# A fixed group of four dense fp32 matmuls at the start of each RWKV scan of a hybrid FNet / RWKV-7 step

## The chip, the cores and the metric

The kernel runs on one core of one Trainium2 chip. The metric is the device time of one execution in microseconds (us). Three runs of the kernel before gave 3294.38, 3295.61 and 3301.01 us; the median is 3295.61 us.

## The reference, cut to what matters

One layer is computed for two streams, 1024 latent tokens and 128 prompt tokens, with a model width of 1024: norm, SwiGLU FFN, norm, mixer, norm, FFN, final norm. The mixer has a Fourier half and an RWKV-7 half of 8 heads with 64 features each. The RWKV half is a recurrence over the tokens, forward and backward:

```python
def step(state, inp):
    r_t, w_t, k_t, v_t, kk_t, a_t = inp
    sa = jnp.einsum('bhvk,bhk->bhv', state, -kk_t)
    state = (state * w_t[:, :, None, :]
             + sa[..., None] * (kk_t * a_t)[:, :, None, :]
             + v_t[..., None] * k_t[:, :, None, :])
    return state, jnp.einsum('bhvk,bhk->bhv', state, r_t)
```

The kernel returns both streams' outputs and the final prompt states of both directions.

## The kernel before, in words

The program is a row of stages with a barrier between them: load, modulation, FFN 0, mixer projection, Fourier, RWKV, mixer output, FFN 1, output. RWKV (`rwkv`, L1838) takes the 8 heads in four pairs. For each pair `rw_chunks` (L1461) turns the recurrence into 18 chunks of 64 tokens, `rw_scan` (L1712) runs through the chunks one after the other, and `rw_turn` (L1329) normalises and gates the result and makes the operands of the next pair. The first three pairs are the body of a hardware loop with `more=True`; the fourth stands behind it with `more=False`.

In `rw_scan` both directions d = 0, 1 go through chunks i = 0 to 17 together. TensorE's program per chunk is: `s_part(i, 0)` and `s_part(i, 1)` (L1740: two 64x64 matmuls each, the heads' states times a chunk factor), then `rest(i, 0)` and `rest(i, 1)` (L1749, L1754, L1758: two matmuls each for the new state and four for the output). Every fp32 matmul call stands as two MATMUL instructions in the trace. `s_part` waits for the states of the chunk before (VectorE, L1791) and for ScalarE to have copied the outputs of the chunk before out of PSUM (L1813). `rest` waits for VectorE's sum (L1784). GpSimd multiplies the old state by the decay (L1804) for VectorE's L1791. At i = 0 `s_part` waits for the memset of the states, L1779.

With `more`, class `Prep` prepares the next pair inside the scan: after the chunk's `rest(i, 1)` TensorE runs item i - 1 of a list. The first item, `ss`, is `head_sums` (L1137): nine calls with 128x128 weights and two moving columns. It waits for ScalarE's `sq` (L1230), which follows `kraw` (L1228), which waits for a load and for `ka1` on VectorE (L1255). On VectorE `prep.dve` comes after the chunk's L1791, and on ScalarE `prep.act` comes after the chunk's L1813. The further items are matmuls with 384 moving columns (L1216) and 128x128 ones (L1145). PSUM banks 6 and 7 belong to these items in the scan; the matmuls of the scan itself write banks 0 to 5. Nothing reads bank 7 before the item that writes it.

Of the kernel before, what the change touches and what calls it, by code (L numbers as in the profile page):

```python
# [14 lines left out]
P = 128  # L15
# [31 lines left out]
C_ID, C_MASK, C_ONE, C_BLK, C_CLS = 0, 128, 384, 512, 640  # L47
# [25 lines left out]
def fresh(name, count=count()):  # L73

    return f"{name}{next(count)}"
# [48 lines left out]
def mm3(pe, out, w_hi, w_lo, x_hi, x_lo, start, stop):  # L124

    pe.matmul(out, w_lo, x_hi, start=start, stop=False)  # L126
    pe.matmul(out, w_hi, x_lo, start=False, stop=False)  # L127
    return pe.matmul(out, w_hi, x_hi, start=False, stop=stop)  # L128


def parts(c):
# [1580 lines left out]
def rw_scan(nc, io, sb, rw, zd, p, more):  # L1712
# [6 lines left out]
    with Stage(nc) as st, nc.psum_tensor(fresh("c_ps"), [P, 8, 512], F32) as ps:  # L1719
        pe_t = Steps(st.sem("pe_s"), [x for i in range(NCH) for x in (f"S{i}_0", f"S{i}_1", f"M{i}_0", f"Y{i}_0", f"M{i}_1", f"Y{i}_1")] +  # L1720
                     ["st0", "st1"])
        dve_t = Steps(st.sem("dve_s"), ["zero"] + [x for i in range(NCH) for x in
                                                   [f"S{i}_0", f"S{i}_1"] + [f"M{i}_0", f"M{i}_1"]])
        act_t = Steps(st.sem("act_s"), [f"Y{i}_{d}" for i, d in SD] + ["st0", "st1"])
        pool_t = Steps(st.sem("pool_s"), [f"mp{i}_{d}" for i, d in SD])
        out_s = st.sem("out_s")
        prep = Prep(st, io, sb, rw, zd, p + 1, ps[:, 6:8, :]) if more else None
        old = lambda i, d: rw.m0[:, d, :] if i == NPC else rw.m[:, i % 2, d, :]
        with st.block() as block:
            @block.tensor  # L1730
            def _(pe):

                def s_part(i, d):
                    c = order[d][i]
                    dve_t.wait(pe, f"M{i - 1}_{d}" if i else "zero")
                    if i:
                        act_t.wait(pe, f"Y{i - 1}_{d}")
                    for h in range(2):
                        rows = slice(HS * h, HS * h + HS)
                        last = pe.matmul(ps[0:HS, 2 * d + h, 0:HS], rw.ar[rows, d, 0, c * HS:(c + 1) * HS],  # L1740
                                         old(i, d)[rows], start=True, stop=True)
                    pe_t.did(f"S{i}_{d}", last)

                def rest(i, d):
                    c = order[d][i]
                    dve_t.wait(pe, f"S{i}_{d}")
                    for h in range(2):
                        rows = slice(HS * h, HS * h + HS)
                        last = pe.matmul(ps[rows, 4 + d, 0:HS], rw.bt[:, d, c, HS * h:HS * h + HS],  # L1749
                                         rw.sv[:, d, h, c, :], start=True, stop=True)  # L1750
                    pe_t.did(f"M{i}_{d}", last)
                    for h in range(2):
                        rows = slice(HS * h, HS * h + HS)
                        pe.matmul(ps[rows, 2 * d + h, HS:2 * HS], rw.sv[:, d, h, c, :], rw.gr[:, d, h, c, HS:2 * HS],  # L1754
                                  start=True, stop=False)
                    for h in range(2):
                        rows = slice(HS * h, HS * h + HS)
                        last = pe.matmul(ps[rows, 2 * d + h, HS:2 * HS], old(i, d)[rows],  # L1758
                                         rw.ar[rows, d, 1, c * HS:(c + 1) * HS], start=False, stop=True)
                    pe_t.did(f"Y{i}_{d}", last)  # L1760
                for i, d in SD:
                    s_part(i, d)
                    if d:
                        rest(i, 0)
                        rest(i, 1)
                        if more:
                            prep.pe(pe, i)
                for d in range(2):

                    act_t.wait(pe, f"Y{NCH - 1}_{d}")  # L1770
                    for h in range(2):
                        rows = slice(HS * h, HS * h + HS)
                        last = pe.matmul(ps[rows, 2 * d + h, HS:2 * HS], rw.st[rows, d, :],
                                         sb["cst"][rows, C_ID + HS * h:C_ID + HS * h + HS], start=True, stop=True)
                    pe_t.did(f"st{d}", last)

            @block.vector
            def _(dve):
                dve_t.did("zero", dve.memset(rw.m[:, 0, :, :], 0.0))  # L1779
                for i in range(NCH):  # L1780
                    for d in range(2):
                        c = order[d][i]
                        pe_t.wait(dve, f"S{i}_{d}")
                        dve_t.did(f"S{i}_{d}", dve.tensor_tensor(rw.sv[0:HS, d, :, c, :], ps[0:HS, 2 * d:2 * d + 2, 0:HS],  # L1784
                                                                 rw.gr[0:HS, d, :, c, 0:HS], ALU.add))
                    for d in range(2):
                        c = order[d][i]
                        new = rw.st[:, d, :] if i == NPC - 1 else rw.m[:, (i + 1) % 2, d, :]
                        pe_t.wait(dve, f"M{i}_{d}")
                        pool_t.wait(dve, f"mp{i}_{d}")  # L1790
                        dve_t.did(f"M{i}_{d}", dve.scalar_tensor_tensor(new, ps[:, 4 + d, 0:HS], rw.pc[:, d, c:c + 1],  # L1791
                                                                       rw.mp[:, d, :], ALU.mult, ALU.add))
                    if more:
                        prep.dve(dve, i)

            @block.gpsimd
            def _(pool):
                for i, d in SD:
                    c = order[d][i]
                    if i:  # L1800
                        dve_t.wait(pool, f"M{i - 1}_{d}")
                    else:
                        dve_t.wait(pool, "zero")
                    pool_t.did(f"mp{i}_{d}", pool.tensor_scalar(rw.mp[:, d, :], old(i, d), rw.pc[:, d, c:c + 1], None, ALU.mult))  # L1804

            @block.scalar
            def _(act):
                for i, d in SD:
                    c = order[d][i]
                    pe_t.wait(act, f"Y{i}_{d}")  # L1810
                    for h in range(2):
                        rows = slice(HS * h, HS * h + HS)
                        last = act.activation(y[d][rows, c * HS:(c + 1) * HS], ps[rows, 2 * d + h, HS:2 * HS], ACT.Copy)  # L1813
                    act_t.did(f"Y{i}_{d}", last)
                    if more and d:
                        prep.act(act, i)
                for d in range(2):
                    pe_t.wait(act, f"st{d}")
                    dve_t.wait(act, f"M{NCH - 1}_{d}")
                    for h in range(2):  # L1820
                        rows = slice(HS * h, HS * h + HS)
                        last = act.activation(rw.mp[rows, d, :], ps[rows, 2 * d + h, HS:2 * HS], ACT.Copy)
                    act_t.did(f"st{d}", last)

            @block.sync
            def _(sp):
                if more:
                    prep.sync(sp)
                    for sem in prep.z_in + prep.w_in:
                        sp.wait_ge(sem, 16)  # L1830
                for d, name in enumerate(("state_f", "state_b")):
                    act_t.wait(sp, f"st{d}")
                    sp.dma_start(io[name][0, 0, bass.ds(p * 2, 2), :, :].rearrange("h v k -> (h v) k"), rw.mp[:, d, :])\
                      .then_inc(out_s, 16)
                sp.wait_ge(out_s, 32)
# [129 lines left out]
```

## Time and profile before

| | |
|---|---|
| median of the three runs | 3295.61 us |
| the runs | 3294.38 to 3301.01 us |
| span of the profiled execution, first to last instruction | 3298.7 us |
| TensorE matmul busy (PE) | 2845.0 us, 86% |
| VectorE busy (DVE) | 1469.7 us, 45% |
| ScalarE busy (ACT) | 782.5 us, 24% |
| mean granted clock of TensorE | 0.850 of full |

No separate time is given for the profiled execution. Its span, 3298.7 us, lies 3.1 us above the median and inside the runs' own spread, so what lies around the span is not told apart here, and sums are made as differences. In the profile PE is TensorE's matmuls, PEld its weight loads, PEclk the granted clock as a share of full speed (1.0 is 2.4 GHz, 0.5 is 1.2 GHz). Matmuls are pipelined: the duration of one has a tail that the next one overlaps, so the pace is read from the starts.

### The profile page before, as it was taken

How to read it: one execution, taken by the hardware profiler on the slowest of the kernel's cores; microseconds unless marked ns; L12 is line 12 of the kernel's file. 1: busy time of each engine (PE TensorE's matmuls, PEld its weight loads, DVE VectorE, ACT ScalarE, POOL GpSimd, SP SyncE). 2: the span in 40 equal slices, each digit the busy share in tenths (PEclk: the TensorE clock that was granted, in tenths of full speed). 3: DMA queues.
4: the chain of work that ended last, by engine and by line, in shares of the span. 5: the costliest groups of instructions: out<-in, count | busy, mean ns of one | idle time of the engine just before them, and what ended most of it. 6: DMA issues, size and time to landing. Idle time of an engine off the chain costs nothing. (4 is left out here: it accounts for less than half of the span.)

```text
span 3298.7 us, 47247 instructions
## 1 busy us (share of the span) xinstructions
PE 2845.0 (86%) x18910; PEld 2646.2 (80%) x18910; DVE 1469.7 (45%) x2799; ACT 782.5 (24%) x1527; POOL 105.5 (3%) x165
## 2 busy tenths in 40 slices
PE   4589999999995999578679678686879999999995
PEld 2289999999995998266476565665879999999995
DVE  1453333333437661372563745723364433333335
ACT  1231111112104111333233433322141111111112
POOL 0000000000000000001102001010000000000000
PEclk8799999999997999665665755757989999999997
DMA  8511111111101223110010110104111111111101
GB/s 342 211 52 39 38 38 49 40 45 45 45 0 40 95 82 112 68 28 26 18 23 24 25 39 3 30 9 161 33 51 45 42 40 38 38 38 51 38 19 58
DMA packets 190797, 182.67 MB, mean 55 GB/s; under 512 B 43955, under 2 KB 163550, under 8 KB 190686
## 3 DMA queue, kind: packets, MB, share of 16 engines
q1 hardware_dynamic: 190416, 180.97, 17.0%
q8 instruction: 86, 1.41, 0.2%
q14 instruction: 25, 0.20, 0.0%
q10 hardware_dynamic: 270, 0.09, 0.0%
HBM read 153.05 MB, written 27.98 MB: 55 GB/s over the span
## 5 line engine op out<-in xcount | busy, mean ns | idle before, releaser
L126 PE MATMUL ff_ps<-h_hi,ff_wlo 128*128 128x384 f32 x2112 | 710.7, 336 | 12.2 <-ACT ff_s L591 7.7
L127 PE MATMUL ff_ps<-h_lo,ff_whi 128*128 128x384 f32 x2112 | 709.4, 336 | 0.0
L128 PE MATMUL ff_ps<-h_hi,ff_whi 128*128 128x384 f32 x2112 | 709.1, 336 | 0.0
L126 PEld LDWEIGHTS ff_ps<-h_hi,ff_wlo 128*128 128x128 f32 x2112 | 399.9, 189 | 13.4 <-issue 8.2
L639 DVE TENSOR_TENSOR ff_s<-ff_ps,ff_s 128x384 f32<-128x384 f32 x132 | 73.6, 557 | 752.6 <-PE ff_ps L128 751.3
L127 PEld LDWEIGHTS ff_ps<-h_lo,ff_whi 128*128 128x128 f32 x2112 | 399.8, 189 | 0.0
L128 PEld LDWEIGHTS ff_ps<-h_hi,ff_whi 128*128 128x128 f32 x2112 | 399.4, 189 | 0.0
L128 PE MATMUL ff_ps<-ff_uhi,ff_whi 128*128 128x384 f32 x1056 | 352.7, 334 | 0.0
L126 PE MATMUL ff_ps<-ff_uhi,ff_wlo 128*128 128x384 f32 x1056 | 352.7, 334 | 0.0
L127 PE MATMUL ff_ps<-ff_ulo,ff_whi 128*128 128x384 f32 x1056 | 352.7, 334 | 0.0
L591 ACT ACTIVATE ff_s<-ff_ps 128x384 f32<-128x384 f32 x132 | 64.9, 492 | 740.9 <-PE ff_ps L128 740.9
L650 DVE SCALAR_TENSOR_TENSOR x_again<-ff_ps,mod,x_again 128x256 f32<-128x256 f32 (+1 forms) x352 | 171.0, 514 | 72.1 <-PE ff_ps L128 71.4
L650 DVE SCALAR_TENSOR_TENSOR x<-ff_ps,mod,x 128x256 f32<-128x256 f32 (+1 forms) x352 | 170.9, 513 | 72.2 <-PE ff_ps L128 71.5
L595 ACT ACTIVATE ff_uhi<-ff_s 128x384 fp32r<-128x384 f32 x132 | 69.5, 526 | 556.4 <-DVE ff_s L639 556.4
L126 PEld LDWEIGHTS ff_ps<-ff_uhi,ff_wlo 128*128 128x128 f32 x1056 | 198.2, 188 | 0.0
L127 PEld LDWEIGHTS ff_ps<-ff_ulo,ff_whi 128*128 128x128 f32 x1056 | 198.2, 188 | 0.0
L128 PEld LDWEIGHTS ff_ps<-ff_uhi,ff_whi 128*128 128x128 f32 x1056 | 198.2, 188 | 0.0
L632 DVE TENSOR_TENSOR ff_wlo<-ff_raw,ff_whi 128x1024 fp32r<-128x1024 f32 x132 | 157.5, 1219 | 17.7 <-ACT ff_whi L586 17.5
L126 PE MATMUL pj_ps<-h_hi,pj_wlo 128*128 128x384 f32 x456 | 155.4, 341 | 7.4 <-DVE h_lo L454 7.4
L127 PE MATMUL pj_ps<-h_lo,pj_whi 128*128 128x384 f32 x456 | 154.7, 339 | 0.0
L128 PE MATMUL pj_ps<-h_hi,pj_whi 128*128 128x384 f32 x456 | 154.6, 339 | 0.0
L586 ACT ACTIVATE ff_whi<-ff_raw 128x1024 fp32r<-128x1024 f32 x132 | 131.9, 1044 | 0.0
(267 smaller groups left out, 3735.3 us busy)
## 6 DMA issues: line engine op xcount, KB each, us to landing
md_w<-w_mod SPq DMA_DIRECT2D x9, 4096.0 KB, 25.5
ff_raw<-ffn_w_gate SPq DMA_DIRECT2D x44, 512.0 KB, 4.5
ff_raw<-ffn_w_up SPq DMA_DIRECT2D x44, 512.0 KB, 3.9
ff_raw<-ffn_w_down SPq DMA_DIRECT2D x44, 512.0 KB, 3.7
pj_raw<-w_in SPq DMA_DIRECT2D x19, 512.0 KB, 4.0
z_dram<-pj_zo SPq DMA_DIRECT2D x15, 576.0 KB, 2.9
rw_rkv<-z_dram SPq DMA_DIRECT2D x12, 576.0 KB, 5.4
x_dram<-x SPq DMA_DIRECT2D x1, 4608.0 KB, 22.7
```

Of the source, the lines that this page charges most:

```text
L126: pe.matmul(out, w_lo, x_hi, start=start, stop=False)
L127: pe.matmul(out, w_hi, x_lo, start=False, stop=False)
L128: return pe.matmul(out, w_hi, x_hi, start=False, stop=stop)
L586: act.activation(w_hi[:, u, :], raw[:, u % RAW, :], ACT.Copy).then_inc(w_hi_s, 1)
L591: act.activation(silu[:, t % 2, :], ps[:, t % 2, 0:CW], ACT.Silu).then_inc(gate_free, 1)
L595: act.activation(hid_hi[:, m, c * CW:(c + 1) * CW], hid[:, t % 2, :], ACT.Copy).then_inc(hid_hi_s, 1)
L632: dve.tensor_tensor(w_lo[:, u, :], raw[:, u % RAW, :], w_hi[:, u, :].bitcast(F32), ALU.subtract)\
L639: dve.tensor_tensor(hid[:, t % 2, :], ps[:, 2 + t % 2, 0:CW], silu[:, t % 2, :], ALU.mult)\
L650: last = dve.scalar_tensor_tensor(xs, ps[:, 4 + n % 4, a:b], sb["mod"][:, (3 * (2 * f) + 2) * KD + o, s:s + 1], xs, ALU.mult, ALU.add)
```

## The change

A function is added, and called once in TensorE's program of each scan, ahead of the first `s_part`. It multiplies constants (the first 512 columns of the constant tile, by the identity in it), four times over into PSUM bank 7, each with `start=True`.

```diff
+def keep_clock(pe, sb, out, n):
+
+    for _ in range(n):
+        pe.matmul(out, sb["cst"][:, C_ID:C_ID + P], sb["cst"][:, 0:512], start=True, stop=True)
...
                     pe_t.did(f"Y{i}_{d}", last)
+                keep_clock(pe, sb, ps[:, 7, :], 4)
                 for i, d in SD:
                     s_part(i, d)
```

## Rows read from the trace of the kernel before

**Rows 1.** The page: busy time, granted clock in 40 slices

```profile
PE 2845.0 (86%) x18910; PEld 2646.2 (80%) x18910; DVE 1469.7 (45%) x2799; ACT 782.5 (24%) x1527; POOL 105.5 (3%) x165
...
PEclk8799999999997999665665755757989999999997
```

**Rows 2.** Stretches of the first, third and fourth scan: length, busy us (instructions), clock, DMA share, GB/s

```profile
1510.60:1594.20 83.60, 78.02 (x644) 52.27 (x644) 30.63 (x87) 32.08 (x94) 21.83 (x36) 0.50 0.07 24
...
1954.30:2038.00 83.70, 77.98 (x644) 52.30 (x644) 30.92 (x88) 32.17 (x95) 21.82 (x36) 0.50 0.07 24
2175.60:2236.00 60.40, 50.35 (x584) 38.74 (x584) 20.48 (x73) 16.59 (x76) 15.97 (x36) 0.50 0.01 3
```

**Rows 3.** Timeline, fourth scan, one chunk: start, us, engine, line, tile, count

```profile
2195.40 0.48 PE L1740 MATMUL c_ps<-rw_m,rw_ar 64*64 64x64 f32 x4 [0.43 <-DVE rw_sv L1784]
...
2197.63 0.32 PE L1758 MATMUL c_ps<-rw_ar,rw_m 64*64 64x64 f32 x2
...
2197.99 0.45 ACT L1813 ACTIVATE rw_work<-c_ps 64x64 f32<-64x64 f32 x2 [0.58 <-PE c_ps L1758]
...
2198.59 0.48 PE L1740 MATMUL c_ps<-rw_m,rw_ar 64*64 64x64 f32 x4 [0.43 <-DVE rw_sv L1784]
```

**Rows 4.** Timeline, chunk stage, 64x64 matmuls at the full clock, then at the low one

```profile
2114.65 4.41 PE L1587 MATMUL g_ps<-rw_sv,rw_gr 64*64 64x64 f32 x72
...
2136.14 7.83 PE L1607 MATMUL g_ps<-rw_sv,rw_wt 64*64 64x64 f32 x71
```

**Rows 5.** Timeline, wide fp32 matmuls: L946 at the full clock, L1367 and L1216 low

```profile
1309.28 3.60 PE L946 MATMUL fo_ps<-fo_tab,fo_t 128*128 128x512 f32 x8
...
1600.80 4.04 PE L1367 MATMUL p_ps<-rw_work,cst 128*128 128x384 f32 x6 [6.59 <-DVE rw_work L1411]
...
1589.41 0.84 PE L1216 MATMUL c_ps<-rw_lora,rw_w 64*128 64x384 f32 x1
```

**Rows 6.** Stretches around the L1367 matmuls of Rows 5 (columns as Rows 2)

```profile
1601.20:1604.50 3.30, 3.30 (x6) 1.78 (x6) 2.66 (x3) 1.66 (x2) 0.00 (x0) 0.50 0.01 2
1604.60:1607.90 3.30, 2.59 (x11) 1.37 (x9) 3.02 (x3) 1.63 (x2) 0.00 (x0) 1.00 0.00 0
```

**Rows 7.** Timeline, opening of the first scan

```profile
1510.41 0.17 DVE L1779 MEMSET rw_m<- 128x128 f32 x1 [2.51 <-PEq L116]
...
1510.63 0.69 PE L1740 MATMUL c_ps<-rw_m,rw_ar 64*64 64x64 f32 x8 [2.06 <-DVE rw_m L1779]
...
1513.68 0.45 ACT L1813 ACTIVATE rw_work<-c_ps 64x64 f32<-64x64 f32 x2 [0.58 <-PE c_ps L1758]
...
1514.75 1.25 ACT L1228 ACTIVATE rw_kk<-rw_rkv,rw_pn 128x1152 f32<-128x1152 f32 x1 [0.62 <-DMA rw_rkv<-z_dram]
...
1516.04 1.16 ACT L1230 ACTIVATE rw_sq<-rw_kk 128x1152 f32<-128x1152 f32 x1
...
1517.26 4.00 PE L1137 MATMUL c_ps<-cst,rw_sq 128*128 128x2 f32 x18 [0.43 <-ACT rw_sq L1230]
1521.19 0.37 PE L1740 MATMUL c_ps<-rw_m,rw_ar 64*64 64x64 f32 x2
```

**Rows 8.** Timeline, turn stage: the same L1137 at the full clock

```profile
1607.48 2.17 PE L1137 MATMUL p_ps<-cst,rw_work 128*128 128x2 f32 x18 [0.71 <-ACT rw_work L1390]
```

**Rows 9.** Stretches of the Fourier stage, one-column matmuls from 1297.3 on (columns as Rows 2)

```profile
1297.40:1300.70 3.30, 3.30 (x29) 3.24 (x27) 0.00 (x0) 0.60 (x1) 0.00 (x0) 1.00 1.02 423
1300.80:1304.10 3.30, 2.95 (x14) 2.87 (x13) 0.17 (x1) 0.00 (x0) 0.00 (x0) 0.50 0.49 201
```

**Rows 10.** Stretches of the chunk stage, 64x64 matmuls at either clock (columns as Rows 2)

```profile
2113.20:2116.50 3.30, 3.30 (x45) 3.10 (x44) 2.99 (x10) 3.30 (x11) 0.00 (x0) 1.00 0.00 0
2116.60:2119.90 3.30, 2.46 (x43) 2.32 (x40) 2.79 (x13) 2.28 (x5) 0.00 (x0) 1.00 0.25 71
2120.00:2123.30 3.30, 0.00 (x0) 0.00 (x0) 2.96 (x11) 0.00 (x0) 0.00 (x0) 0.50 0.48 88
...
2143.90:2147.20 3.30, 3.30 (x67) 3.30 (x66) 0.06 (x1) 1.47 (x3) 0.00 (x0) 0.50 0.33 94
```

## The prediction, before the changed kernel was run

> **What bounds the kernel now.** The page comes first: TensorE is busy for 86% of the span, and the only run of slices where its clock drops well below full is the middle, from 6 down to 5 tenths; that is the RWKV part [rows 1]. The stretches of the scans show the granted clock at 0.50 from first to last (the second, not shown, reads like the first), so 3 x 83.6 + 60.4 = 311 us of scanning run at 1.2 GHz [rows 2]. PE counts as busy for 78.0 of 83.6 us there, but that is not throughput.
>
> One chunk of the fourth scan shows what the time is made of [rows 3]. From one start of the second direction's `s_part` (2195.40) to the next (2198.59) it is 3.19 us. The loop runs: `s_part`, both `rest`, the last L1758 pair ends at 2197.63 + 0.32 = 2197.95, ScalarE copies until 2198.44, and TensorE starts again at 2198.59. So 0.64 us are ScalarE and hand-over, which no TensorE clock touches, and 2.55 us are TensorE in a chain. The scans lie alone on the path: barriers stand before and behind, and TensorE's program is in order. Whatever is put ahead of the first `s_part` is on the path in full, and a faster clock is a gain on the path.
>
> **The cost of the four matmuls.** Two L1740 parts, four calls, stand as 8 MATMULs [rows 7], so four calls make 8 instructions of 128x512. At the full clock eight such instructions take 3.60 us with the tail of the last [rows 5]; without the tail I take 3.4. At the low clock six of 384 columns take 4.04, and a single one there 0.84, so they start (4.04 - 0.84) / 5 = 0.64 apart [rows 5], so 512 columns take 0.85 and 8 take 6.8 us. These are the bounds. The clock rises on the way: L1367 starts at 1600.80 at 0.50 and the stretch from 1604.60 has 1.00 [rows 5, 6], some 3.8 us of dense work. I take 4 us: 4.0 at the low clock do 4.0 / 0.85 = 4.7 instructions, the other 3.3 take 1.4 us, together 5.4. The memset hid 1510.63 - 1510.41 = 0.2 us of this [rows 7], which leaves **5.2 us per scan**, 20.8 for four. Nothing else covers it: VectorE and ScalarE wait for the first matmuls of the scan, and GpSimd's first product is used only after them. SP's loads at the scan's start are not moved and land during the burst, but the preparation that they feed gains nothing from that, as follows.
>
> **What the full clock gives back, per chunk.** A chunk has 16 calls, 32 instructions, and the two heads' instructions run side by side, 16 pairs; all but the first direction's two `s_part` pairs, 14, lie in the 2.55 us. 64x64 matmuls in a row take 4.41 / 72 = 0.061 us each at the full clock and 7.83 / 71 = 0.110 at the low one [rows 4]. 14 x 0.049 = 0.69. The tail of the last, 0.32 at the low clock [rows 3], I let shrink by 0.09 (an estimate), and the four places where the shape of the weights switches leave gaps of about 0.14 us, which I let shrink by 0.05 each (an estimate; bounds none and half). Sum 0.69 + 0.09 + 0.20 = 0.98, so about **1.0 us per chunk**, 3.19 to 2.2. Bounds: 0.69 if only the columns go faster, 1.28 if all of the TensorE part halves.
>
> **How long it lasts in the first three scans.** Before, the second chunk is followed by `ss` at 1517.26 and the third chunk starts at 1521.19, that is 10.56 us after 1510.63 [rows 7]. With the full clock, from the end e of the burst: `ka1` and the ScalarE copies ahead of `kraw` end about 2.5 us after e (before: 1513.68 + 0.45 - 1510.63 = 3.5, less one chunk's gain) [rows 7]. `kraw` was bound by its load before, at 1514.75; now the load is long in and it waits in ScalarE's queue behind the first chunk's copies. `kraw` and `sq` take 1.25 + 1.16, so `ss` starts at e + 5.0, although both chunks are through at about e + 4.2. `ss` is 18 instructions with two moving columns each: 3.93 us at the low clock [rows 7], 2.1 at the full one [rows 8]. And it is the kind of work after which the clock falls: in the Fourier stage PE was busy 3.30 of 3.30 us with one-column matmuls at clock 1.00, and the stretch behind it has 0.50, without any idle time of TensorE between [rows 9]. So I expect the fall during `ss` and grant it 0.8 us of gain. The third chunk then starts at e + 5.0 + 3.9 - 0.8 = e + 8.1, and with e 5.2 us late this is 13.3 after the old start: 13.3 - 10.56 = +2.8 us. From there the scan runs at 0.50 as before, because its own work did not raise the clock in any of the scans [rows 2]. Three scans: **+8.3 us**. Bounds: 3 x (3.2 - 2.5), if the burst costs 3.4, to 3 x 6.6, if nothing is given back.
>
> **The fourth scan** has no `ss`. It pays 5.2. What comes back hangs on how long 64-wide matmuls with gaps keep the clock. The nearest rows are the chunk stage [rows 10]: with 45 MATMULs of 64 and 128 columns and no gap the clock stayed; behind a stretch in which the 64x64 ones ran out (2.46 us busy of 3.30) it fell. The scan at the full clock would have gaps of some 0.6 us in each 2.2 us chunk, between the two. And 67 of the 64x64 ones without any gap did not raise it [rows 10]. I take a fall after some two to three chunks, 2.5 us back: **+2.7 us**.
>
> **The sum.** 8.3 + 2.7 = +11.0 us, on the median 3295.6: **3307 us**. The difference is formed within one execution, whose span lies 3.1 us above the median; so does the level the reader would see in a span. What measurement can tell from no change is about 0.2%, 6.6 us.
>
> **The rivals.**
>
> *The fourth scan keeps the clock.* Then 18 x 1.0 = 18 us come back there, -12.8 instead of +2.7, and the total is 8.3 - 12.8 = -4.5: 3291 us, not slower than before. The place is the loop of [rows 3], and it decides if the clock outlasts its ScalarE gap. For it speaks that the stretch with 45 matmuls kept it; against, the fall after the 43 [rows 10]. 0.23. In part of this (1.2 us per chunk) it ends below -6.6.
>
> *All four scans keep the clock*, `ss` included. Each of the first three gains 18 x 1.0 for the chunks and, of the 83.6 - 60.4 = 23.2 us by which the preparation lengthens it [rows 2], at most half, 11.6; less 5.2 that is -24. Total 3 x -24 - 12.8 = -85: 3211 us. The scans' TensorE idles for only 5.6 of 83.6 us [rows 2], which speaks for it; the one-column stretch of [rows 9], where it idled for nothing and the clock fell, speaks against. 0.04. The Trainium skill, "TensorE: Matmul & The Clock Gate", section "Why this matters for your kernels", says that to avoid drops in mid-kernel one should leave no long idle gaps of TensorE between bursts of matmuls; by that rule this rival is what happens, since no gap here is long. By the trace it is not enough.
>
> *The burst raises nothing, or the gain is nil.* 4 x 6.6 = +26: 3322 us. L1367 with six instructions did raise the clock [rows 5, 6], and the burst has more columns; what could be is that the rise comes only at its end and goes at once. 0.08.
>
> *The matmuls cost nothing visible*, because their result is unread or they fit before the scan opens. Nothing drops an instruction in this program, and the room ahead of L1740 is 0.2 us. 0.02: 3296 us.
>
> **The numbers.** The forecast has 0.60 and spans some 3300 to 3313 (burst 4.4 to 6.4 us, fall in the fourth scan after none to six chunks); the rest, 0.03, is scatter. The range must reach the fourth-scan rival, so it goes from 3290 to 3316. Faster: all four, 0.04, a third of the fourth-scan rival, 0.07: 0.11. Same: the rest of that rival 0.16, the light end of the forecast 0.08, no cost 0.02, and 0.01 of scatter: 0.27. Slower: 0.62.
>
> **What would show it.** Right: each scan opens with 8 MATMULs of 128x512 over 4.5 to 6.5 us; PEclk reaches 1.00 toward their end and falls back during L1137 in the first three scans; L1740 opens about 5 us after the memset; scans 1 to 3 are 2 to 4 us longer, the stages between unchanged. Wrong: PEclk at 1.00 beyond L1137 in any of the first three, or chunk periods of 2.2 us through the fourth scan; a burst of 6.8 us with the clock at 0.50 throughout; L1740 chunks that don't shorten although the clock is 1.00.

## The result, and the profile after

The changed kernel takes 3312.1 us (median of four runs, 3307.91 to 3316.7), against 3294.99 before. The ratio is 1.0046, interval 1.0032 to 1.006: +15 us, between +10 and +20 (the two medians lie 17 apart). The sign of the forecast (3307, +11) holds, and so does its mechanism, a group that costs more than the short stretch of full clock behind it gives back. The first three scans lengthened by more than the sum had, and the cause of the fall was told too simply; both are taken up below.

The page of the changed kernel, TensorE's busy time and the granted clock in 40 slices. They look like [rows 1]; one number in the tenths differs here and there, and nothing in them tells what the change did.

```profile
PE 2860.8 (87%) x18942; PEld 2648.0 (80%) x18942; DVE 1470.5 (44%) x2799; ACT 782.4 (24%) x1527; POOL 105.5 (3%) x165
...
PEclk7799999999997999665665755657989999999997
```

So the next view is that of [rows 2], here for the four scans of the changed kernel (length, busy us and count per engine, clock, DMA share, GB/s). The mean clock went from 0.50 to 0.54 or 0.55, which is one short piece at full speed in each; the first three windows are cut at the old length, 83.6 us, and hold 614 to 619 instead of 644 matmuls although 8 were added: the scan no longer fits.

```profile
1504.50:1588.10 83.60, 78.23 (x614) 50.11 (x614) 28.45 (x82) 30.19 (x87) 21.83 (x36) 0.54 0.07 24
1730.40:1814.00 83.60, 78.25 (x614) 50.21 (x616) 28.45 (x82) 30.20 (x87) 21.84 (x36) 0.54 0.07 24
1956.80:2040.40 83.60, 78.24 (x619) 50.63 (x620) 28.45 (x82) 30.47 (x88) 21.83 (x36) 0.54 0.07 24
2180.40:2242.90 62.50, 54.23 (x592) 39.33 (x592) 20.46 (x73) 16.60 (x76) 15.96 (x36) 0.55 0.01 2
```

The opening of the first scan in the timeline (start, us, engine, line, tile, count) answers to [rows 7]. The eight instructions of the group (L134) take 6.13 us, and the first L1746, the old L1740, starts at 1510.58, 6.0 us after the memset instead of 0.2. `kraw` (L1234) waits in ScalarE's queue behind the copies, and `ss` (L1143) starts 5.1 us after the first L1746.

```profile
1504.52 6.13 PE L134 MATMUL c_ps<-cst 128*128 128x512 f32 x8 [1.78 <-PEq L116]
1504.57 0.17 DVE L1786 MEMSET rw_m<- 128x128 f32 x1 [2.51 <-PEq L116]
...
1510.58 0.45 PE L1746 MATMUL c_ps<-rw_m,rw_ar 64*64 64x64 f32 x8
...
1513.18 1.26 ACT L1234 ACTIVATE rw_kk<-rw_rkv,rw_pn 128x1152 f32<-128x1152 f32 x1
...
1514.46 1.16 ACT L1236 ACTIVATE rw_sq<-rw_kk 128x1152 f32<-128x1152 f32 x1
...
1515.68 3.46 PE L1143 MATMUL c_ps<-cst,rw_sq 128*128 128x2 f32 x18 [0.77 <-ACT rw_sq L1236]
```

The same scan in stretches: low while the group starts, 1.00 from its last instructions through the first two chunks, 0.50 again from 1516.3, which is 0.6 us after the start of `ss`.

```profile
1506.10:1509.40 3.30, 3.30 (x5) 1.35 (x4) 0.00 (x0) 0.00 (x0) 0.00 (x0) 0.50 0.97 344
1509.50:1512.80 3.30, 3.03 (x39) 1.70 (x37) 1.21 (x6) 0.53 (x3) 0.54 (x2) 1.00 0.53 199
1512.90:1516.20 3.30, 2.22 (x36) 1.76 (x33) 1.13 (x4) 3.17 (x7) 1.14 (x3) 1.00 0.01 2
1516.40:1519.60 3.20, 3.20 (x21) 3.16 (x21) 0.18 (x1) 0.17 (x1) 0.00 (x0) 0.50 0.02 5
```

In the third scan the clock is down at 1966.87, 0.2 us before `ss` starts, and `ss` runs at the low clock from its first matmul:

```profile
1963.50:1966.80 3.30, 2.50 (x44) 1.81 (x42) 1.65 (x7) 3.02 (x6) 1.73 (x4) 1.00 0.05 17
1966.90:1970.20 3.30, 3.12 (x15) 3.13 (x15) 0.00 (x0) 1.00 (x5) 0.00 (x0) 0.50 0.02 5
```

```profile
1967.08 4.00 PE L1143 MATMUL c_ps<-cst,rw_sq 128*128 128x2 f32 x18 [0.77 <-ACT rw_sq L1236]
```

The fourth scan has no `ss`, and the clock falls all the same, at 2192.1. In the two stretches at 1.00 the chunks take 2.26 us (from the second-direction L1746 at 2189.15 to that at 2191.41) instead of 3.19 [rows 3].

```profile
2185.40:2188.70 3.30, 3.03 (x39) 1.74 (x37) 1.05 (x4) 0.58 (x3) 0.58 (x2) 1.00 0.02 5
2188.80:2192.10 3.30, 2.68 (x48) 2.05 (x46) 1.73 (x7) 1.08 (x5) 1.09 (x3) 1.00 0.00 0
2192.20:2195.50 3.30, 2.87 (x36) 2.22 (x34) 1.27 (x5) 0.87 (x4) 0.92 (x3) 0.50 0.00 0
```

```profile
2189.15 0.33 PE L1746 MATMUL c_ps<-rw_m,rw_ar 64*64 64x64 f32 x4 [0.31 <-ACT rw_work L1820]
...
2190.82 0.45 ACT L1820 ACTIVATE rw_work<-c_ps 64x64 f32<-64x64 f32 x2 [0.20 <-PE c_ps L1764]
...
2191.41 0.33 PE L1746 MATMUL c_ps<-rw_m,rw_ar 64*64 64x64 f32 x4 [0.31 <-DVE rw_sv L1791]
```

Scan by scan, read from one profiled execution of each kernel, those of the experiments below among them (e1 to e11): the start of the first L1740 (or its successor), and the length of the scan, both from the memset on, the length to the end of the last copy of the states; and how long the clock was at 1.00, counted from the memset.

| kernel | first `s_part` | scans 1, 2, 3 | scan 4 | at 1.00, scans 1 to 3 | at 1.00, scan 4 |
|---|---|---|---|---|---|
| before | 0.2 | 84.3, 83.9, 83.8 | 58.9 | never | never |
| the change | 6.0, 5.7, 5.2, 6.0 | 88.0, 88.0, 87.8 | 62.4 | 4.9-11.7, 4.3-11.2, 3.2-10.1 | 4.9-11.7 |
| e1_one | 1.9 | 85.5, 85.5, 85.5 | 45.4 | never | 3.7-41.3 |
| e2_eight | 9.5, 9.3, 9.5, 9.1 | 91.5, 91.4, 91.5 | 65.7 | 4.9-15.2, 4.6-14.8, 5.0-15.2 | 4.2-14.4 |
| e3_burst_fill | 6.5, 6.0, 5.1, 6.2 | 98.5, 98.5, 95.6 | 48.9 | 5.9-12.8, 4.9-11.8, 3.1-13.3 | 5.3 to the end |
| e4_fill | 0.2 | 94.7, 94.7, 94.7 | 63.3 | never | never |
| e5_all_full | 6.5, 6.3, 5.9, 6.4 | 84.4, 84.3, 81.7 | 48.9 | 5.8-22.9, 5.5-22.6, 4.7-21.8 and 28.6-35.4 | 5.6 to the end |
| e6_wide_ss | 6.2, 6.6, 6.2, 5.9 | 84.3, 84.4, 84.3 | 56.7 | 5.2-22.3, 6.1-23.1, 5.2-22.3 | 4.6-25.1 |
| e7_fourth | 0.2 (scan 4: 5.0) | 84.4, 83.9, 83.8 | 47.5 | never | 2.8 to the end |
| e8_fourth_burst | 0.2 (scan 4: 5.0) | 84.3, 84.0, 83.8 | 50.7 | never | 3.0-37.1 |
| e9_fill_prep | 6.1, 6.2, 6.4, 6.1 | 69.2, 69.4, 78.4 | 48.6 | to the end, to the end, 5.8-53.6 | 5.0 to the end |
| e10_fill_prep_two | 3.6 | 69.8, 76.7, 85.8 | 46.1 | 12.5 to the end, 5.3-32.6 and 36.1-53.1, 5.5-32.8 | 3.7 to the end |
| e11_fill_waits | 6.4, 6.4, 6.3, 6.2 | 70.0, 70.0, 69.9 | 48.7 | 5.6 to the end, three times | 5.3 to the end |

In the change's profile the four scans are 3.7, 4.1, 3.9 and 3.5 us longer than in that of before, together 15.3 us, and that is the whole of the measured +15. The two spans differ by 7.4 us only, since in this execution everything ahead of the first scan took 5.8 us less than in the one of before (memset at 1504.57 against 1510.41), with no line changed there, and all that lies between and behind the scans took another 2.1 us less.

### The profile page after: what moved, and what is told of

The parts are those of the page before. It is cut to its first block and busy times, and to the rows that moved or that the text cites. A ratio compares the mean times of both kernels' runs of the same rounds, so it can differ in the third digit from the quotient of the medians.

```text
span 3306.1 us, 47311 instructions
## 1 busy us (share of the span) xinstructions
PE 2860.8 (87%) x18942; PEld 2648.0 (80%) x18942; DVE 1470.5 (44%) x2799; ACT 782.4 (24%) x1527; POOL 105.5 (3%) x165
```

## The experiments

All were made on the changed kernel. On the chips they ran on, the kernel before was run beside them; each ratio is against those runs.

**One matmul, and eight.** The call's last argument was 1 in one kernel and 8 in the other.

```diff
-                keep_clock(pe, sb, ps[:, 7, :], 4)
+                keep_clock(pe, sb, ps[:, 7, :], 1)
```

> One constant matmul ahead of each scan instead of four. My theory (the group costs its own length, at the low clock until the clock rises, and gives back what the two or three chunks behind it gain): two instructions of 0.85 us at the low clock less 0.2 us hidden, no rise of the clock, nothing given back: +1.5 us per scan, +6 us over before (ratio 1.0018). Rival A (any start of dense work wakes the clock and the cost is that of the waking): clock at 1.00 behind it, about the same +15 us as with four. Rival B (the cost lies in something other than the matmuls, such as bank 7 or the loads): +15 us.

Measured: 3305.8 us (ten runs) against 3303.0, ratio 1.0009, 0.9998 to 1.0021. The first three scans are as expected: no rise, 1.2 to 1.7 us longer. The fourth, in the profiled execution, did what nothing in my theory had: the clock rose behind a single matmul, and stayed at 1.00 for 37.6 us, almost to the end. That scan took 45.4 us instead of 58.9. The stretches of the first and the fourth scan:

```profile
1506.10:1591.70 85.60, 79.94 (x646) 52.76 (x646) 31.33 (x88) 32.52 (x96) 21.81 (x36) 0.50 0.07 23
2176.10:2221.60 45.50, 39.12 (x586) 28.37 (x586) 20.38 (x73) 16.60 (x76) 15.97 (x36) 0.91 0.01 2
```

This execution took 3285.67 us, one other 3294.87, and the remaining eight 3300.7 to 3310.3, which suggests that a long hold is rare here; only the first of them has a trace. So the fourth scan's work is neither clearly too thin nor clearly dense enough; that became the question of the further runs.

> Eight constant matmuls instead of four. My theory: the four more run at the full clock, 4 x 2 x 0.43 = 3.4 us per scan, +13.8 us over the change, and the clock falls as soon after the end of the group as before (about 5 us), so nearly the same is given back: about +29 us over before (ratio 1.0088). Rival (a longer dense stretch makes the clock last longer in the scan): the clock stays at 1.00 for more than 7 us behind the group, or through the fourth scan, and the total is then at or below that of the change.

Measured: 3327.6 us, ratio 1.0072, 1.0055 to 1.0089, that is +24 us where +29 was expected. The group of 16 instructions takes 9.20 us in the fourth scan, where the 8 took 6.12 in the same scan of the change, and the first three scans are 3.5 us longer than with four: the added matmuls cost their length at the full clock, and the clock falls as soon behind the group as before (5.3 to 5.7 us after the first `s_part`). The rival, that a longer dense stretch makes the clock last, falls.

**A filler in every chunk**, with the group and without it. In the second kernel the call of `keep_clock` is gone.

```diff
                 for i, d in SD:
                     s_part(i, d)
+                    if d == 0:
+                        fill(pe, sb, ps[:, 4, P:2 * P])
...
+def fill(pe, sb, out):
+    pe.matmul(out, sb["cst"][:, C_ID:C_ID + P], sb["cst"][:, C_BLK:C_BLK + P], start=True, stop=True)
```

> The change, and one more constant matmul of 128 columns per chunk, between the two s_part, where TensorE waits for ScalarE (about 0.5 us idle at either clock; the matmul takes 0.21 us at full). My theory (the clock falls because the chunks at full speed leave TensorE too little to do, not because of ss alone): the fourth scan runs at 1.00 to its end, chunk period 2.3 us instead of 3.19, the scan 16 us shorter than before less the 5.8 of the group; the first three fall at ss (two-column matmuls) and stay low: +4 us each. Total about +12 - 10 = +2 us. Rival (what counts is that there is no long idle gap): the filler changes nothing, the clock falls 6 us behind the group in the fourth scan as well, total as with the change, +15 us.

Measured: 3330.5 us, ratio 1.008, 1.0063 to 1.0097, +26 us where +2 was expected. The statement on the fourth scan is right to the microsecond, that on the first three is not. First the two kinds of scan, the first and the fourth, in stretches:

```profile
1512.70:1611.30 98.60, 96.44 (x688) 62.39 (x688) 32.44 (x88) 32.56 (x96) 21.75 (x36) 0.53 0.06 20
2216.50:2265.50 49.00, 48.08 (x628) 33.90 (x628) 20.25 (x73) 16.53 (x76) 15.89 (x36) 0.95 0.01 2
```

The fourth is at 1.00 to its end, with a chunk every 2.29 us. The first three got the filler at the low clock, and in them it is not hidden: the preparation item stands between L1758 and the next `s_part`, so ScalarE's copy is long done when TensorE asks for it, and there is no gap to fill. Chunks of 4.51 us became 5.18. In the third scan the clock outlasted the two-column `ss`, which took 2.17 us there, and fell 0.7 us behind it: `ss` does not always bring it down.

> The filler of 128 columns per chunk alone, without the group of four. My theory: at the low clock it takes 0.43 us, about what the gap has (0.43 us idle before the second s_part), so it costs 0 to 0.1 us per chunk, 0 to +7 us in all; with the more dense items of the preparation (L1145) the clock may rise for a while in the first three scans, up to -5 us each; in the fourth it does not rise. Rival (the filler by itself wakes the clock): the fourth scan at 1.00 within some us, 15 us shorter.

Measured: 3335.0 us, ratio 1.0094, 1.0077 to 1.0111. The clock stays at 0.50 in all four scans; the filler neither raises it nor is it free at the low clock (94.7 instead of 84, 63.3 instead of 58.9). Both of my cost figures were wrong, for the reason above and because even in the fourth scan it takes 0.22 us per chunk more than the gap gives (chunks of 3.41 us instead of 3.19). What the pair settles, for the fourth scan: the same filler keeps the clock at 1.00 for 44 us where a group has raised it, and does nothing for it where none has.

```profile
1509.10:1603.90 94.80, 93.11 (x680) 62.55 (x680) 32.46 (x88) 32.56 (x96) 21.75 (x36) 0.50 0.06 21
2203.00:2266.40 63.40, 62.29 (x620) 47.30 (x620) 20.54 (x73) 16.53 (x76) 15.90 (x36) 0.50 0.01 2
```

**What part `ss` had.** Its nine calls get 128 moving columns instead of two. Each call's surplus columns are overwritten by the next call or unread.

```diff
+def wide_sums(pe, sb, ps, x):
+    blk = sb["cst"][:, C_BLK:C_BLK + P].rearrange("p (h j) -> p j h", h=2)
+    for t in range(NT):
+        last = pe.matmul(ps[:, 2 * t:2 * t + P].rearrange("p (j h) -> p j h", h=2), x[:, t * P:(t + 1) * P], blk,
+                         start=True, stop=True)
+    return last
```

> The change, and in the first three scans ss with 128 moving columns instead of two, nothing else. It tells what part ss had in the fall. If ss was the cause, as the prediction says: the clock survives it wherever the two chunks before it held, and the rest of that scan is at 1.00 (25 to 30 us shorter). If the thin chunks before ss were enough, as the fourth scan hints: it falls at about the same time in most scans; but ss itself is now dense and may raise it again, which then holds in the chunks with preparation. In either case at least some scans of 84 us become 55 to 60. Only if the chunks with preparation cannot hold the clock are all three as with the change, +4 us each.

Measured: 3300.6 us (ten runs) against 3300.1, ratio 1.0003, 0.9989 to 1.0016. The clock survives `ss` in all three scans and falls 10 us later, at 22.3, 23.1 and 22.3 instead of 10.1 to 11.7; these scans are 84.3 us instead of 88. The ten executions, 0.4% below the change by the two ratios, say that this is not peculiar to the profiled one. So a dense `ss` keeps the clock, and the two-column one had a part in the fall. It was not the only cause: in the third scan of the change the clock had gone before `ss` began, and the fourth lost it without any. What the fall needs besides, or how often the chunks do it alone, three scans cannot say. And 55 to 60 us did not come: there is a second thin place behind it. The first scan in stretches, and what ScalarE and TensorE do there:

```profile
1519.20:1521.60 2.40, 2.40 (x21) 2.23 (x21) 0.00 (x1) 0.49 (x3) 0.00 (x0) 1.00 0.04 7
1521.70:1526.40 4.70, 4.16 (x67) 2.81 (x63) 2.17 (x9) 3.17 (x7) 1.33 (x3) 1.00 0.00 0
1526.50:1530.00 3.50, 2.58 (x32) 1.55 (x34) 1.94 (x6) 3.41 (x8) 0.82 (x2) 0.98 0.00 0
1530.10:1533.50 3.40, 3.23 (x26) 1.73 (x24) 0.81 (x4) 1.43 (x6) 0.45 (x1) 0.50 0.02 5
```

```profile
1524.07 1.28 ACT L1265 ACT_TABLE_LOAD   x1
...
1525.97 1.28 ACT L1255 ACT_TABLE_LOAD   x1
...
1527.39 0.91 ACT L1835 ACTIVATE rw_work<-c_ps 64x64 f32<-64x64 f32 x4
1527.96 0.81 PE L1761 MATMUL c_ps<-rw_m,rw_ar 64*64 64x64 f32 x8 [0.72 <-ACT rw_work L1835]
1528.31 1.28 ACT L1265 ACT_TABLE_LOAD   x1
```

ScalarE changes its table three times for the preparation (sigmoid, square root, sigmoid) and holds back the scan's copies. At the low clock this was covered (chunks of 4.50 to 4.51 us there, as elsewhere); at the full clock TensorE waits for it, and a chunk takes 3.78 us where the one ahead took 2.84. ScalarE is busy for 3.41 of 3.50 us there and TensorE starts 32 matmuls, against 67 in the 4.70 us ahead. Behind it the clock falls. That this stretch is the cause is so far an inference; e9 tries it.

**All of it, first try.** `wide_sums`, the filler in the fourth scan's chunks from 1 on, and in the first three scans one filler in chunk 1 and one of 384 columns ahead of `ss`.

```diff
+                    if d == 0 and i and (i == 1 or not more):
+                        fill(pe, sb, ps[:, 4, P:], P)
                     if d:
                         rest(i, 0)
                         rest(i, 1)
+                        if more and i == 1:
+                            fill(pe, sb, ps[:, 7, :], 384)
```

> The change, plus what should keep TensorE's clock up: in the first three scans the nine calls of ss get 128 moving columns instead of two (the surplus columns are overwritten or unread), one constant matmul of 128 columns ahead of the second s_part of chunk 1 and one of 384 columns ahead of ss, where TensorE waits for ScalarE; in the fourth scan the filler of 128 columns in every chunk. My theory (the clock falls where the work is thin, in the chunks without preparation and in ss, and the later chunks with preparation are dense enough at full speed): all four scans run at 1.00 to near their end, chunk period with preparation 2.5 us instead of 4.5, the first three scans about 55 us instead of 84, the fourth 49 instead of 59: about -97 us, 3205 against 3303 (ratio 0.971). Rival (the chunks with preparation cannot hold it either): the clock falls after ss, the first three scans cost +4 us each, the fourth -10: about +2 us.

Measured: 3286.7 us (ten runs) against 3300.1, ratio 0.9959, 0.9945 to 0.9972. The fourth scan does as expected, 48.9 us; the first three lose the clock at 22.9, 22.6 and 21.8, in the same place as above, and I had not seen it. -13 us instead of -97. That one scan of the three had a second piece at 1.00 (28.6 to 35.4), behind the dense L1145 items, fits the reading that the dense items can raise it (L1165 in this kernel; the first of them starts 1.5 us before the rise).

**The fourth scan alone.** With the group and the filler:

```diff
-                keep_clock(pe, sb, ps[:, 7, :], 4)
+                if not more:
+                    keep_clock(pe, sb, ps[:, 7, :], 4)
...
+                    if d == 0 and i and not more:
+                        fill(pe, sb, ps[:, 4, P:], P)
```

> The group of four and the 128-column filler per chunk in the fourth scan alone; the first three as before the change. My theory: fourth scan 49 us instead of 59 at clock 1.00, nothing else moved: -10 us (ratio 0.997). Rival (the first three scans or what they leave behind matter to the fourth): the clock does not rise or falls early, +3.5 us.

Measured: 3287.9 us (ten runs, 3285.2 to 3293.5), ratio 0.9969, 0.9959 to 0.9979: -10 us, as said. The profiled scan is 11.4 us shorter.

```profile
2170.20:2217.80 47.60, 46.39 (x626) 33.16 (x626) 20.20 (x73) 16.60 (x76) 15.99 (x36) 0.97 0.01 2
```

With the group but no filler:

> The group of four in the fourth scan alone, no filler: one part of the change. My theory: this scan holds the clock only by chance (it fell 6 us behind the group in the profile of the change, and held 37 us in the profile with one matmul), so the runs fall in two groups, +3.5 us and -12 us against before. Rival (the hold with one matmul has to do with the single matmul, not with chance): all runs at +3.5 us.

Measured: 3296.2 us (twelve runs), ratio 0.9989, 0.9971 to 1.0007. Not two groups but a spread: 3277.4 to 3305.5, where the kernel with the filler, on the same chip, spans 8 us. The profiled execution (3293.5) held the clock to 32 us behind the first `s_part` and then lost it; in other profiles the same work held it to 5.3, 5.7, 19 and 39 us behind it (e2, the change, e6, e1). The plain chunks of the scan can keep the full clock and often do not, and the fall came at a different chunk in each case but two. A long hold does not need the single matmul. What decides between these executions of the same work stays open.

**The filler where TensorE waits.** As the first try, but in the first three scans the filler stands ahead of each preparation item.

```diff
             bank = self.ps[:, n % 2, :]
+            if self.wide:
+                for _ in range(3 if i in (1, 3, 4) else 1):
+                    fill(pe, self.sb, bank[:, CW:], P)
```

> As e5_all_full, but in the first three scans the filler stands ahead of every preparation item: one constant matmul of 128 columns, three of them ahead of ss and in chunks 3 and 4, where TensorE waits for ScalarE's table loads. My theory (in e6 and e5 the clock fell at +22 us because ScalarE's three table loads stall the chunks 3 and 4 and leave TensorE too little work, and would be held with work there): the first three scans run at 1.00 from the group to their last chunk, chunk period 3.0 to 3.1 us instead of 4.5, about 62 us instead of 84; the fourth 49 instead of 59: -66 - 10 = -76 us, ratio 0.977. Rival (the full clock is taken back about 17 us after it rises, whatever TensorE does in these scans): fall at +22 again, and the fillers cost 0.4 us per chunk at the low clock: the first three scans 89 us or more, total about +5 us.

Measured: 3247.2 us against 3297.8, ratio 0.9858, 0.9823 to 0.9893: about -50 us by the medians where -76 was expected. Three of the four scans are at 1.00 from the group to the end; the third lost the clock at 53.6:

```profile
1505.00:1574.30 69.30, 61.21 (x698) 41.11 (x698) 30.85 (x88) 32.30 (x96) 21.29 (x36) 0.96 0.09 29
1712.90:1782.30 69.40, 61.37 (x698) 41.20 (x698) 30.81 (x88) 32.30 (x96) 21.28 (x36) 0.96 0.08 29
1920.70:1999.10 78.40, 70.77 (x698) 46.70 (x698) 31.20 (x88) 32.41 (x96) 21.26 (x36) 0.80 0.07 25
2133.10:2181.70 48.60, 47.46 (x626) 33.46 (x626) 20.18 (x73) 16.60 (x76) 15.98 (x36) 0.95 0.01 2
```

The rival, that the full clock is taken back some 17 us after it rises whatever TensorE does, falls: it lasts 64 us here. A scan of the kind is 69.3 us instead of my 62, since at the full clock the chunks with preparation take 3.26 us, not 3.05, and four of them take longer: 3.71 twice, with three fillers and ScalarE's table loads, and 4.55 and 4.03, with waits for VectorE. The clock passed the place of the table loads in all three scans, where in e5 and e6 it fell in six of six; that carries the reading of the second thin place.

> As e9_fill_prep, with two constant matmuls at the start of each scan instead of four. My theory: where the clock rises after the two (3.4 us of dense work) the scan is about 2 us shorter than with four; where it does not, it rises at the dense ss, some 10 us into the scan, and is held from there, with 3 to 5 us lost against four; in the fourth scan it rises or not by chance. Total within 10 us of e9_fill_prep. Rival (only the group at the start can raise it): whole scans at 0.50, 90 us each, and the total above before.

Measured: 3266.0 us, ratio 0.9887, 0.9851 to 0.9924. By the medians that is 19 us above the kernel with four, outside what I had given; by the ratios it is 10, and with four runs each the two intervals overlap, so a difference is not shown. In the first scan the two did not raise the clock and it rose at 12.5, at the dense `ss`, and the scan was still 69.8 us; but the second and the third lost it at 32.6 and 32.8, some 1.6 us behind the 1.73 us in which chunk 7 waits for VectorE. That is another place where holding was not sure; whether the shorter group had a part in it, or chance, these few runs don't tell. The rival is out: the clock does rise without the group of four.

**Filler in the two long waits for VectorE as well.**

```diff
-                for _ in range(3 if i in (1, 3, 4) else 1):
+                for _ in range(3 if i in (1, 3, 4, 6, 12) else 1):
```

> As e9_fill_prep, with three instead of one filler also ahead of the items of chunks 6 and 12; the chunks behind them have TensorE waiting for long VectorE work of the preparation (1.7 us in the first case), and in the profile of e9_fill_prep the third scan lost the clock in the second of these places, at +53.6. My theory: the extra work lies in waits and costs under 1 us per scan, and the clock survives all four scans in nearly every run: the third scan 69 to 70 us like the first two instead of 78, total 3240 against 3298 before (ratio 0.983), with a narrower spread than e9. Rival (the loss in the third scan had another cause): scans of 78 us still occur, ratio at e9's 0.986 or above.

Measured: 3248.4 us (five runs, 3241.0 to 3249.0) against 3300.5, ratio 0.9836, 0.9823 to 0.985: 54 us faster than before and, by the two ratios (0.9836 / 1.0046 = 0.979), some 69 us faster than the change. No run of the five is above 3249, and in the profiled execution all four scans hold the clock, the third among them:

```profile
1929.60:1999.60 70.00, 62.36 (x706) 42.14 (x706) 30.89 (x88) 32.31 (x96) 21.29 (x36) 0.96 0.08 28
```

The added fillers did not all land in waits. TensorE's wait in chunk 7 of the first scan is the same in e9 (first line) and here (second), and the way there from chunk 6 grew from 4.55 to 5.00 us: they stand ahead of the L1165 matmuls that VectorE waits for, so VectorE's work, and with it the wait, only moved back. Ahead of chunk 13 they did fill: the wait went from 1.01 to 0.57 us, and the chunk stayed at 4.03.

```profile
1538.07 0.34 PE L1773 MATMUL c_ps<-rw_sv,rw_bt 128*64 128x64 f32 x4 [1.73 <-DVE rw_sv L1811]
```

```profile
1546.92 0.34 PE L1773 MATMUL c_ps<-rw_sv,rw_bt 128*64 128x64 f32 x4 [1.73 <-DVE rw_sv L1811]
```

Whether these fillers made the third scan hold is not shown: two of e9's three such scans held without them, three of its four runs were at 3243 to 3247, and the two kernels' intervals overlap.

## Why the prediction was right, and where it was off

*The group lies on the path in full.* Right. The first `s_part` starts 6.0, 5.7, 5.2 and 6.0 us after the memset instead of 0.2: 5.5 us a scan on average, where the sum had 5.2.

*The clock rises on the way.* Right: at 4.9, 4.3, 3.2 and 4.9 us, with 4 taken. With one matmul it did not rise in three scans of four.

*A chunk at the full clock gains 1.0 us.* 3.19 to 2.26, 0.93. The bounds held.

*In the first three scans the clock falls during `ss`.* Nearly right in place: it fell 0.6 and 0.3 us after `ss` began in the first two scans, and 0.2 us before it in the third. In cause it was half right: with `ss` made dense and nothing else touched the clock lasted to 22 us, so `ss` had a part, but the third scan and the fourth show that the chunks ahead of it, with TensorE busy for 2.2 to 2.7 of 3.3 us, can be enough. The size was off. I granted `ss` 0.8 us of gain; its 18 matmuls took 3.46, 3.72 and 4.00 us instead of 4.00, a gain of 0.5, 0.3 and none. And I took the first scan for all three: there, before the change, `ss` had waited for a late load and started 6.8 us after the memset, in the second and third 6.4 and 6.3, so some 0.45 us that I counted as given back was there only once. Term for term: +2.8 forecast, +3.7, +4.1 and +3.9 measured. These are the two mis-sized steps, "grant it 0.8 us of gain" and the use of 10.56 for every scan, worth 1.6 and 0.9 us over the three scans. The group's 0.2 us more in each of them on average, and 0.1 us more from its end to `ss`, make up the rest of the 3.5 us between +8.3 and +11.8.

*The fourth scan.* +2.7 forecast, +3.5 measured: 5.8 us of delay, 2.3 back. That this came so close is in part luck: the same scan, with the group ahead of it, was 2.2 us shorter than before in the profile of e6 and 8.2 shorter in that of e8, and over e8's twelve runs it brought -4 us by the ratio (between -10 and +2).

*The rival of the fourth scan that keeps the clock* was no rival but a part of the spread: it happens, for some chunks or nearly to the end, and it did not in the profiled execution of the change. The 0.23 given to it was for an all or nothing that these runs do not show. The profiled execution of the change, with a short hold in this scan, is the fastest of its four (3307.9), so the other three give no sign of a longer one.

*All four keep the clock* did not happen, although no gap of TensorE in the opening is longer than 0.8 us. The Trainium skill's rule ("TensorE: Matmul & The Clock Gate", section "Why this matters for your kernels", to leave no long idle gaps) is not enough here, as [rows 9] had shown: the clock was lost at two-column matmuls with TensorE busy, and at small ones with short waits between them. The experiments show the other half of it: with work in those places all four scans kept the clock (e11). They were then some 14 us shorter each in the first three, not the 24 that the rival had put, since chunks with preparation take 3.26 us or more at the full clock.

## What to carry to other kernels

A clock that is raised by a group of dummy matmuls is worth only what the work behind it keeps; read first whether that work, at its full-speed pace, leaves TensorE thin, because a faster engine meets waits (here ScalarE's table loads and VectorE's preparation) that its slow pace had covered. A dummy matmul is free only in a wait, and not ahead of a matmul whose result the awaited engine itself needs; look for the wait in the variant of the loop that it goes into, since the same line was hidden in one scan and cost 0.67 us per chunk in the other three. And where one variant of a loop is profiled three times, read all three before taking the first for the rest.

## What the runs showed that I had not expected

The same 64-wide chunks, with the same waits, held the full clock to anything between 5 and 39 us behind the first `s_part`; one dummy matmul of 128 columns per chunk made it last in each of the six profiled fourth scans that had one and a group ahead of it. A single matmul of 512 columns, 2.04 us at the low clock, was followed by a rise of the clock in one of the four scans of e1's profile, 1.8 us into the chunks; without any, no scan of before or of e4 had a rise. And the part of the program ahead of the first scan, the same in all of these kernels, took 1504.6 to 1513.6 us to its memset in thirteen profiles: a difference of up to 9 us between two spans says nothing by itself, and it was the lengths of the scans that told the change apart.
